# Folding the modulation sums by 24 small matmuls on TensorE in place of 48 small operations on VectorE, in a four-layer transformer forward pass

## The chip, the cores and the metric

The kernel runs on one core of a Trainium2 chip. The metric is the device time of one execution in microseconds (us), lower is better. Five engines work beside each other and meet only through semaphores: TensorE (PE in the profile, with its weight loads as PEld), VectorE (DVE), ScalarE (ACT), GpSimd (POOL), and SyncE (SP), which issues nearly all DMAs here.

## The reference

A batch of one with 256 tokens of width 1024 goes through two blocks of two layers each. The first block ("one" in the kernel) takes its scales, shifts and gates from a conditioning vector `c`:

```python
cond = jax.nn.silu(c)                                  # 1 x 1024
for l in range(2):
    mod = cond @ ada_w[l] + ada_b[l]                   # 1024 -> 9 * 1024
    sh1, sc1, g1, sh2, sc2, g2, sh3, sc3, g3 = jnp.split(mod, 9, axis=-1)
    hn = _modulate(_rms_norm(h, norm_g[l, 0]), sh1, sc1)
    h = h + 0.5 * g1 * _swiglu(hn, ffn1_w_in[l], ffn1_w_out[l])
    hn = _modulate(_rms_norm(h, norm_g[l, 1]), sh2, sc2)
    z = hn @ w_in[l]     # four mixers: differential attention, convolution, gated MLP, forgetting attention
    h = h + g2 * (mixed @ w_out[l])
    hn = _modulate(_rms_norm(h, norm_g[l, 2]), sh3, sc3)
    h = h + 0.5 * g3 * _swiglu(hn, ffn2_w_in[l], ffn2_w_out[l])
```

The second block ("two") has two layers of attention of three kinds and an MLP, with no such modulation. Everything is float32. The change is in how `mod` is summed up, in block one alone.

## The kernel before

**Layout.** The activations `h` lie with the model's 1024 channels on the partitions, as 8 tiles of 128 x 256 tokens. A vector of 1024 numbers, such as `sh1`, is then 8 columns of 128. `mod` of one layer is 72 such columns: 0 to 16 are `sh1, sc1`, 16 to 48 `g1, sh2, sc2, g2`, 48 to 64 `sh3, sc3`, 64 to 72 `g3`.

**Weight products.** Weights stream from HBM in chunks of 256 columns into a ring of four slots. To multiply float32 numbers in TensorE's faster float32r form, ScalarE rounds each chunk into `w_hi` (L1217), GpSimd subtracts it from the original into `w_lo` (L683), each in two halves, and TensorE does three matmuls, hi by hi, hi by lo and lo by hi, for each tile (L717). Two chunks' worth of `w_hi` and `w_lo` are held, so a half is rounded as soon as TensorE has used the one two chunks before. The lines L748 to L752 are the same product for the first chunks of a stage, where it goes tile by tile as the normed input appears.

**Stages of a layer of block one**, in this order: `f1` in (22 chunks in 11 pairs, p = 0 to 10), `f1` out (16 chunks, g = 0 to 3), `z` (the products for the four mixers, 12 chunks), the mixers themselves, `o` (4 chunks), `f2` in and `f2` out. Between two stages stands a norm: `norm_sum` on TensorE (L833, L836) sums the squares, ScalarE takes the root (L1251, L1253), and `scale_norm` on VectorE (L1703, L1712) and ScalarE (L1277) make the normed tiles `hn` and `hn_lo` one by one, 8 of them, for which TensorE waits. Each engine runs its own program in a fixed order written out by hand, and waits on counters such as `vector_done`.

**The modulation.** `ada_w` comes in chunks of 512 columns (2 MB). But for the first four of layer 0, VectorE multiplies and adds a chunk over its 8 tiles (`partial_sum`, L1608 to L1613), transposes 32 x 32 blocks (L1624) and reduces them (L1626), which leaves 16 columns in `ada_columns` in which four groups of 32 partitions hold four partial sums of each output. These must still be added across the groups. `ADA_BATCHES` puts the chunks in three batches a layer: chunks 4 to 11, 12 to 15, and 16 to 21 (the last four of these belong to the next layer). `ada_fold` does a batch on VectorE: four copies (L1639) bring each group of 32 partitions to partitions 0 to 31 in `ada_quarters`, four reduces (L1645) add them and write each quarter of the 128 outputs to its own partitions in `ada_folded`. `modulation` (L1659) then adds the bias from `par_all` and writes `mod`. `gated_scale` (L1718) makes `(1 + scale) * gain` of it.

**Where the folds stand.** Batch 0 is folded behind the last pair of `f1` in, batch 1 behind `scale_norm` of `z`, and batch 2 in front of pair 9 of `f2` in. Behind batch 1's fold VectorE has, at the start of `z`: `modulation(48, 64)`, a `gated_scale`, and the splitting of the forget gate's small weights, `wf_parts` and then `wf_hi` and `wf_lo` in full (L1898, L1900, L1903). Modulation columns 0 to 16 of layer 1 are added at the start of that layer, behind `f2` out of layer 0, just before `gated_scale(0, 8)` and `scale_norm("f1")`.

The bank of PSUM numbered 7 is used by the first chunks' sums (`ada_reduce`, L846, four float32 matmuls a chunk with one column each), by the convolution's taps in `z` and by the heads' outputs in the attention. A float32 matmul stands in the trace as two records, each with a weight load of its own: the eight matmuls of `ada_reduce` are 16 records of L846.

Of the kernel before, what the change touches and what calls it, by code (L numbers as in the profile page):

```python
# [20 lines left out]
ALU = mybir.AluOpType  # L21
ACT = mybir.ActivationFunctionType
AX = mybir.AxisListType
# [34 lines left out]
def constant_tables():  # L58
# [3 lines left out]
    def put(name, a):  # L62
        at[name] = sum(p.shape[1] for p in parts)
        parts.append(np.asarray(a, np.float32).reshape(P, -1))
# [6 lines left out]
    put("group32", r[:, None] // 32 == r[None, :] // 32)  # L71
    put("group64", r[:, None] // 64 == r[None, :] // 64)
    put("neg_suffix", -(r[:, None] >= r[None, :]).astype(np.float32))
    put("neg_ones", -np.ones((P, P)))
# [165 lines left out]

def ada_place(c):

    return (c + ADA_CHUNKS if c < ADA_FIRST else c) - ADA_FIRST

# [139 lines left out]
def build(nc, dram, out, at, old):  # L385

    plan = Plan()
    with ExitStack() as ctx:
# [22 lines left out]
        ident_r, unseen = sb("ident_r", P, dtype=F32R), sb("unseen", P, dtype=F32R)  # L411
        arena_start = sb("arena_start", 48)
        arena = sb("arena", ARENA)
# [19 lines left out]
        ada_columns = view(ARENA - 2048, sum(n for _, n in ADA_BATCHES) * 16)  # L433
        ada_quarters = view(ARENA - 2048 + 288, 4, 128)
        ada_folded = view(ARENA - 2048 + 800, sum(n for _, n in ADA_BATCHES) * 4)
        wf_hi, wf_lo = rounded("wf_hi", 0, KT, P), rounded("wf_lo", KT * P, KT, P)
# [261 lines left out]
        def _(pe):  # L698
# [140 lines left out]
            def ada_reduce(layer, c):  # L839
# [7 lines left out]
                last.then_inc(ada_reduced, 1)  # L847

            pe.wait_ge(tables_in, 32)
            turn(bank[:, 4, 0:KT], rows_c[0:KT], "c turned")  # L850
# [45 lines left out]
            def ffn(s, layer, following):  # L896
                for p in range(PAIRS):
                    for r in range(2):
                        b = bank[:, 2 * (p % 2) + r].rearrange("p (c s) -> p c s", c=2)
                        free = ((silu_done, f"{s} hi {p - 2}") if r else (parts_done, f"{s} gated {p - 2}"),)  # L900
                        product(s + "in", (2 * p + r,), (b[:, 0], b[:, 1]), first=s if p == r == 0 else None,
                                free=free if p >= 2 else ())
                for g in range(4):
                    out_product(s + "out", tuple(range(4 * g, 4 * g + 4)), gated,
                                (bank[:, out_bank(g, 0), 0:S], bank[:, out_bank(g, 1), 0:S]), f"{s} out {g}",
                                ((vector_done, f"h {following} {2 * g - 4}"), (vector_done, f"h {following} {2 * g - 3}"))
                                if g >= 2 else ((parts_done, f"{s} gated {PAIRS - 2}"),) if g == 0 else (),
                                f"{s} gated {PAIRS - 1}" if g == 0 else None)
# [89 lines left out]
            for layer in eng.layers("one"):  # L998
# [3 lines left out]
                ffn("f1", layer, "z")  # L1002
                norm_sum("z")
                if layer == 0:
                    pe.wait_ge(params_in, 16 * n_params_total)
# [589 lines left out]
        def _(dve):  # L1595
# [19 lines left out]
            def ada_sum(layer, c):  # L1615

                loads = (ADA_CHUNKS * layer + c - ADA_FIRST) // 2 + 1
                dve.wait_ge(ada_in[c % 2], 16 * loads)
                dve.wait_ge(vector_done, eng.at())
                n, place = ada_sums(layer, c), ada_place(c)  # L1620
                part, turned_ = bank[:, 5 + c % 2], bank[:, 6 - c % 2]
                partial_sum(n, ada[:, c % 2], part, part)
                dve.wait_ge(ada_summed, n + 1)
                dve.transpose(turned_, part).then_inc(vector_done, eng.step())  # L1624
                dve.wait_ge(vector_done, eng.at())
                dve.tensor_reduce(ada_columns[:, 16 * place:16 * (place + 1)],  # L1626
                                  turned_.rearrange("p (b r) -> p b r", r=32), AX.X, ALU.add) \
                    .then_inc(vector_done, eng.step(f"ada columns {place + ADA_FIRST}"))

            def ada_fold(layer, batch):  # L1630

                c, n = ADA_BATCHES[batch]
                if batch == 2 and layer + 1 == L:
                    n = 2
                place = c - ADA_FIRST
                dve.wait_ge(vector_done, eng.at(f"ada columns {c + n - 1}"))
                for q in range(4):
                    dve.tensor_copy(ada_quarters[0:32, q, 0:16 * n],  # L1639
                                    ada_columns[32 * q:32 * q + 32, 16 * place:16 * (place + n)]) \  # L1640
                        .then_inc(vector_done, eng.step())
                dve.wait_ge(vector_done, eng.at())
                terms = ada_quarters[0:32, :, 0:16 * n].rearrange("p g (x q) -> p q x g", q=4)
                for q in range(4):
                    dve.tensor_reduce(ada_folded[32 * q:32 * q + 32, 4 * place:4 * (place + n)], terms[:, q],  # L1645
                                      AX.X, ALU.add).then_inc(vector_done, eng.step())
                dve.wait_ge(vector_done, eng.at())

            def modulation(layer, first, last):

                if layer == first == 0:
                    dve.wait_ge(ada_reduced, 2)
                    dve.wait_ge(tensor_done, eng.at("first ada 3"))
                    sums = bank[:, 7, MOD_TILES:MOD_TILES + last]
                else:
                    place = 4 * ada_place(first // 4)
                    sums = ada_folded[:, place:place + last - first]
                tt(mod[:, first:last], sums, par_all[:, layer, first:last], ALU.add) \  # L1659
                    .then_inc(vector_done, eng.step())  # L1660
                dve.wait_ge(vector_done, eng.at())
# [59 lines left out]
            def ffn(s, gate_at, layer, following):  # L1721
                for p in range(PAIRS):
                    j = p % 2
                    if (s, p) == ("f2", 9):
                        ada_fold(layer, 2)
                        modulation(layer, 64, 72)
                    of = ada_chunk(s + "in", p, layer)
# [9 lines left out]
                if s == "f1":  # L1737
                    ada_fold(layer, 0)
                    modulation(layer, 16, 48)
                ts(der[:, 24:32], mod[:, gate_at:gate_at + 8], 0.5, None, ALU.mult) \  # L1740
# [123 lines left out]
            for layer in eng.layers("one"):  # L1864
                par = par_all[:, layer]
                if layer:
                    dve.wait_ge(vector_done, eng.at())
                modulation(layer, 0, 16)
                gated_scale(0, 8, R_NORM_G).then_inc(vector_done, eng.step())
# [22 lines left out]
                scale_norm("z", lambda k: col(der, 8 + k), 24)  # L1892
                ada_fold(layer, 1)
                modulation(layer, 48, 64)
                gated_scale(16, 56, R_NORM_G + 16).then_inc(vector_done, eng.step())
# [251 lines left out]
```

## Time and profile before

| | |
|---|---|
| time, median of 3 runs | 1983.54 us (1981.48 to 1986.21) |
| the profiled execution's own time | 1986.21 us |
| span of its trace | 1984.4 us |
| PE busy | 96% of the span |
| POOL busy | 69% |
| ACT busy | 48% |
| DVE busy | 44% |

The span runs from the first to the last instruction that the profiler saw; the execution's own time has 1.8 us around it. A busy share says how long an engine had an instruction in it, not how well it used it. Which engine sets the time at a given place is read from the chain of waits: the list, in order of time, of what the last instruction of all was waiting for, followed back to the start.

### The profile page before, as it was taken

The page shows a single profiled execution, that of the slowest core. Times are in us where ns is not written, and L with a number is a line of the kernel's source. Part 1 is how long each engine was busy: PE and PEld are TensorE (multiplying, and loading weights), DVE is VectorE, ACT ScalarE, POOL GpSimd, SP SyncE. Part 2 cuts the span into 40 slices and gives each one's busy share as a digit, 9 for nine tenths or more (in the row PEclk, how much of TensorE's full clock was granted, in tenths as well). Part 3 has the DMA queues.
Part 4 walks back from the last instruction along what each step waited for, and adds up shares of the span by engine and source line. Part 5 has one row for each costly group of instructions (what it writes and reads, how often), then busy time and mean ns, then how long its engine had stood idle before and what let it go on. Part 6 is the DMA issues. An engine that isn't in the chain of part 4 may idle for free.

```text
span 1984.4 us, 36368 instructions
## 1 busy us (share of the span) xinstructions
PE 1908.5 (96%) x15280; PEld 1836.0 (93%) x15280; DVE 880.9 (44%) x1785; ACT 960.8 (48%) x1491; POOL 1362.3 (69%) x628
## 2 busy tenths in 40 slices
PE   6999997999999999889999999999999999999999
PEld 3999995899999998869999998989999999999999
DVE  3675587374137578745121633143311623243322
ACT  2544455344454445444444445646544445646543
POOL 0888770388878887316888865537897865537896
PEclk8999998999999999989999999999999999999999
DMA  9999650595579896317555653436664643346662
GB/s 317 357 347 310 223 191 23 196 367 191 175 268 367 300 304 189 106 44 270 189 161 169 210 168 119 137 122 198 194 210 149 212 149 128 128 147 192 194 204 94
DMA packets 357075, 397.90 MB, mean 201 GB/s; under 512 B 9016, under 2 KB 319024, under 8 KB 356912
## 3 DMA queue, kind: packets, MB, share of 16 engines
q1 hardware_dynamic: 356752, 395.38, 60.1%
q8 instruction: 120, 1.97, 0.4%
q14 instruction: 43, 0.35, 0.1%
q10 hardware_dynamic: 160, 0.20, 0.0%
HBM read 394.51 MB, written 1.05 MB: 199 GB/s over the span
## 4 chain that ended last, share of the span: by engine, by line
PE 88%; DVE 4%; ACT 3%; POOL 1%; SPq 1%; issue 1%; DMA 1%; DVEq 0%; ACTq 0%
PE bank L717 75%; PE bank L803 3%; PE bank L1140 2%; POOL w_lo L683 1%; PE bank L934 1%; PE bank L974 1%; SPq L545 1%; PE bank L748 1%; PE bank L752 1%; PE bank L749 1%; DVE arena L1776 1%; PE bank L708 1%; ACT arena L1353 1%; DVE bank L1703 1%; DMA arena<-in_ada_w 1%
## 5 line engine op out<-in xcount | busy, mean ns | idle before, releaser
L683 POOL TENSOR_TENSOR w_lo<-ring,w_hi 128x1024 fp32r<-128x1024 f32 (+2 forms) x624 | 1362.1, 2210 | 607.2 <-ACT w_hi L1217 606.5
L1217 ACT ACTIVATE w_hi<-ring 128x1024 fp32r<-128x1024 f32 (+2 forms) x624 | 595.2, 978 | 408.0 <-PE bank L717 370.7
L717 PE MATMUL bank<-hn,w_hi 128*128 128x256 f32 x2752 | 774.6, 281 | 4.0 <-POOL w_lo L683 3.0
L717 PE MATMUL bank<-hn_lo,w_hi 128*128 128x256 f32 x2752 | 766.9, 279 | 0.0
L717 PE MATMUL bank<-hn,w_lo 128*128 128x256 f32 x2752 | 766.9, 279 | 0.0
L717 PEld LDWEIGHTS bank<-hn,w_hi 128*128 128x128 f32 x2752 | 519.5, 189 | 8.0 <-POOL w_lo L683 4.8
L717 PEld LDWEIGHTS bank<-hn_lo,w_hi 128*128 128x128 f32 x2752 | 519.2, 189 | 1.1 <-issue 0.5
L717 PEld LDWEIGHTS bank<-hn,w_lo 128*128 128x128 f32 x2752 | 519.6, 189 | 0.0
L717 PE MATMUL bank<-gated,w_hi 128*128 128x256 f32 x1408 | 247.2, 280 | 0.0
L717 PEld LDWEIGHTS bank<-gated,w_hi 128*128 128x128 f32 x1408 | 215.2, 189 | 0.0
L717 PE MATMUL bank<-gated,w_lo 128*128 128x256 f32 x704 | 197.2, 280 | 0.0
L717 PE MATMUL bank<-up,w_hi 128*128 128x256 f32 x1024 | 174.2, 276 | 0.0
L1611 DVE SCALAR_TENSOR_TENSOR bank<-arena,cond,bank 128x512 f32<-128x512 f32 x204 | 154.2, 756 | 7.3
L717 PEld LDWEIGHTS bank<-up,w_hi 128*128 128x128 f32 x1024 | 154.2, 188 | 0.0
L717 PE MATMUL bank<-up,w_lo 128*128 128x256 f32 x512 | 141.3, 276 | 0.0
L717 PEld LDWEIGHTS bank<-gated,w_lo 128*128 128x128 f32 x704 | 133.1, 189 | 0.0
L1732 DVE TENSOR_TENSOR bank<-arena,bank 128x512 f32<-128x512 f32 x44 | 30.6, 696 | 189.1 <-PE bank L717 189.1
L1305 ACT ACTIVATE arena<-bank 128x512 f32<-128x512 f32 x44 | 26.4, 599 | 162.6 <-PE bank L717 162.2
L1353 ACT ACTIVATE arena<-arena,stat 128x128 f32<-128x128 f32 x120 | 53.2, 444 | 89.8 <-DVE stat L1790 39.8
L717 PEld LDWEIGHTS bank<-up,w_lo 128*128 128x128 f32 x512 | 96.1, 188 | 0.0
L1776 DVE CUSTOM_DVE_ANT_0 arena<-bank,const 128x128 f32<-128x128 f32 x120 | 37.5, 354 | 122.7 <-PE bank L934 119.0
L717 PE MATMUL bank<-w_hi,hn 128*128 128x256 f32 x288 | 83.2, 289 | 0.0
(219 smaller groups left out, 2332.2 us busy)
## 6 DMA issues: line engine op xcount, KB each, us to landing
ring<-in_ffn_w_in SPq DMA_DIRECT2D x88, 1024.0 KB, 7.4
ring<-in_w_in SPq DMA_DIRECT2D x72, 1024.0 KB, 5.1
arena<-in_ada_w SPq DMA_DIRECT2D x35, 2048.0 KB, 10.6
ring<-in_w_up SPq DMA_DIRECT2D x32, 1024.0 KB, 5.4
ring<-in_w_down SPq DMA_DIRECT2D x32, 1024.0 KB, 5.1
ring<-in_ffn_w_out SPq DMA_DIRECT2D x32, 768.0 KB, 4.8
ring<-in_ffn_w_out SPq DMA_DIRECT2D x32, 640.0 KB, 4.1
ring<-in_w_in SPq DMA_DIRECT2D x16, 512.0 KB, 3.6
```

Source lines behind the costliest of these rows:

```text
L545: sp.dma_start(dst, src).then_inc(rows_in, 16)
L683: pool.tensor_tensor(w_lo[:, q, ks], ring[:, r, k0:k0 + n], w_hi[:, q, ks], ALU.subtract) \
L708: i = pe.transpose(dst, src, ident[0:n, 0:n])
L717: last = mm(out, a, b, start=start and i == 0, stop=stop and i == 2)
L803: last = mm(outs[c], ring[:, s, k, c * P:(c + 1) * P], x[:, k, :], start=not begun and j == 0, stop=ends and j == len(ks) - 1)
L1140: last = mm(b[:, c], ring[:, s, k0 + k, c * P:(c + 1) * P], o2[:, k0 + k, :], start=(k == 0), stop=(k == nk - 1))
L1217: f(w_hi[:, q, half * 4:half * 4 + n], ring[:, r, k0:k0 + n], ACT.Copy).then_inc(weights_rounded, 1)
L1305: f(act_tmp[:, j], bank[:, 2 * j], ACT.Silu).then_inc(silu_done, eng.step(f"{s} silu {p}", silu_done))
L1353: f(t, t, ACT.Exp, bias=st[:, b + j:b + j + 1], scale=scale, accum_out=st[:, 10 + 2 * m + j:11 + 2 * m + j]) \
L1611: stt(part, src[:, k], col(cond, k), part, ALU.mult, ALU.add).then_inc(vector_done, eng.step())
L1732: tt(bank[:, 2 * j], act_tmp[:, j], bank[:, 2 * j + 1], ALU.mult) \
L1776: dve.tensor_tensor_reduce(out=tile[:, hd.tp[m][0], c0:c1], in0=bank[:, hd.sb[m][0], c0:c1], in1=tab(mask, c1 - c0, c0), scale=1.0, scalar ...
```

## The change

The eight VectorE operations of a fold go. In their place TensorE does four float32 matmuls: the 128 x 128 stationary operand is a window of a new constant table `fold` of 224 columns, which holds a 32 x 32 identity on each group of 32 partitions between 96 columns of zeros on each side; the four windows put the sum over the groups into output partitions 0 to 31, 32 to 63, 64 to 95 and 96 to 127. The moving operand is a quarter of the batch's columns in `ada_columns` (every fourth; 32, 16, 24 or 8 of them). The results stay in PSUM bank 7, and `modulation` reads them there. TensorE does batch 0 between pairs 9 and 10 of `f1` in, batch 2 between pairs 8 and 9 of `f2` in, and batch 1 behind `norm_sum("z")`. VectorE waits for a new count in `ada_reduced` before it adds the bias.

```diff
+    put("fold", np.concatenate([np.zeros((P, 96)), r[:, None] % 32 == np.arange(32)[None, :], np.zeros((P, 96))], axis=1))
...
-        arena_start = sb("arena_start", 48)
+        arena_start = sb("arena_start", 80)
...
-        ada_quarters = view(ARENA - 2048 + 288, 4, 128)
-        ada_folded = view(ARENA - 2048 + 800, sum(n for _, n in ADA_BATCHES) * 4)
...
+            def ada_fold(layer, batch):
+                c, n = ADA_BATCHES[batch]
+                if batch == 2 and layer + 1 == L:
+                    n = 2
+                last_c = c + n - 1
+                pe.wait_ge(vector_done, eng.at(f"ada columns {last_c}"))
+                place = c - ADA_FIRST
+                sums = ada_columns[:, 16 * place:16 * (place + n)].rearrange("p (x q) -> p q x", q=4)
+                for q in range(4):
+                    last = mm(bank[:, 7, 4 * c:4 * (c + n)], tab("fold", P, 96 - 32 * q), sums[:, q],
+                              start=(q == 0), stop=(q == 3))
+                last.then_inc(ada_reduced, 1)
...
+                    if (s, p) in (("f1", 9), ("f2", 8)):
+                        ada_fold(layer, 0 if s == "f1" else 2)
...
                 norm_sum("z")
+                ada_fold(layer, 1)
...
-            def ada_fold(layer, batch):
...
-                for q in range(4):
-                    dve.tensor_copy(ada_quarters[0:32, q, 0:16 * n],
-                                    ada_columns[32 * q:32 * q + 32, 16 * place:16 * (place + n)]) \
-                        .then_inc(vector_done, eng.step())
-                dve.wait_ge(vector_done, eng.at())
-                terms = ada_quarters[0:32, :, 0:16 * n].rearrange("p g (x q) -> p q x g", q=4)
-                for q in range(4):
-                    dve.tensor_reduce(ada_folded[32 * q:32 * q + 32, 4 * place:4 * (place + n)], terms[:, q],
-                                      AX.X, ALU.add).then_inc(vector_done, eng.step())
-                dve.wait_ge(vector_done, eng.at())
...
-                    place = 4 * ada_place(first // 4)
-                    sums = ada_folded[:, place:place + last - first]
-                tt(mod[:, first:last], sums, par_all[:, layer, first:last], ALU.add) \
+                    dve.wait_ge(ada_reduced, ada_batch(*summed)[1])
+                at_ = MOD_TILES if first == 0 else first
+                tt(mod[:, first:last], bank[:, 7, at_:at_ + last - first], par_all[:, layer, first:last], ALU.add) \
```

The three calls of `ada_fold` on VectorE are removed, and the calls of `modulation` name the chunk on which they depend. The constant table grows by 224 columns (112 KB over all partitions); it is among the tables that are loaded during the first pairs of `f1`.

## Rows read from the trace of the kernel before

**Rows 1.** The page: busy time of the engines, then the chain by engine.
```profile
PE 1908.5 (96%) x15280; PEld 1836.0 (93%) x15280; DVE 880.9 (44%) x1785; ACT 960.8 (48%) x1491; POOL 1362.3 (69%) x628
PE 88%; DVE 4%; ACT 3%; POOL 1%; SPq 1%; issue 1%; DMA 1%; DVEq 0%; ACTq 0%
```

**Rows 2.** Chain of waits: start, length (us), engine, line; f2 layer 0, f1 layer 1.
```profile
388.68 180.92 PE bank L717 x1536
...
581.67 174.70 PE bank L717 x1536
```

**Rows 3.** Stretches: busy us of PE, PEld, DVE, ACT, POOL; PEclk, DMA share, GB/s.
```profile
100.00:180.00 80.00, 80.00 (x681) 80.00 (x681) 47.63 (x69) 37.75 (x45) 66.81 (x30) 1.00 1.01 337
...
620.00:700.00 80.00, 80.00 (x708) 80.00 (x708) 49.67 (x70) 38.39 (x46) 70.17 (x32) 1.00 0.96 328
```

**Rows 4.** Chain of waits: float32 matmuls, two groups with full records.
```profile
44.18 0.98 PE bank L846 x8
...
1237.04 0.85 PE bank L934 x4
```

**Rows 5.** Timeline of DVE, last pairs of f1 in, layer 0.
```profile
151.47 0.69 DVE L1626 TENSOR_REDUCE arena<-bank 128x16 f32<-128x512 f32 x1
...
163.69 0.70 DVE L1732 TENSOR_TENSOR bank<-arena,bank 128x512 f32<-128x512 f32 x1 [9.11 <-PE bank L717]
```

**Rows 6.** Chain of waits: starts of z in layer 0 and of block two.
```profile
238.10 0.71 PE bank L836 x2
...
247.54 7.40 POOL w_lo L683 x5
...
1100.69 7.42 POOL w_lo L683 x5
```

**Rows 7.** Timeline of PE at the start of z, layer 0.
```profile
240.98 0.52 PE L748 MATMUL bank<-hn,w_hi 128*128 128x256 f32 x1 [2.19 <-ACT hn L1277]
```

**Rows 8.** Timeline of DVE behind `scale_norm` of z, layer 0.
```profile
247.38 4.00 DVE L1639 COPY arena<-arena 32x64 f32<-32x64 f32 x4
...
252.62 2.34 DVE L1659 TENSOR_TENSOR mod<-arena 128x16 f32<-128x16 f32 x1
254.99 2.31 DVE L1718 SCALAR_TENSOR_TENSOR der<-mod,arena 128x8 f32<-128x8 f32 x1
...
257.65 0.69 DVE L1903 CAST wf_hi<-wf_parts 128x1024 fp32r<-128x1024 f32 x1
```

**Rows 9.** DVE group: busy us, mean ns of one | idle before, releaser.
```profile
L1732 DVE TENSOR_TENSOR bank<-arena,bank 128x512 f32<-128x512 f32 x44 | 30.6, 696 | 189.1 <-PE bank L717 189.1
```

**Rows 10.** Timeline of POOL and PE in the place of rows 8.
```profile
247.54 9.74 POOL L683 TENSOR_TENSOR w_lo<-ring,w_hi 128x512 fp32r<-128x512 f32 x6 [7.63 <-ACT w_hi L1217]
...
254.88 2.40 POOL L683 TENSOR_TENSOR w_lo<-ring,w_hi 128x1024 fp32r<-128x1024 f32 x1
...
257.70 2.90 POOL L683 TENSOR_TENSOR w_lo<-ring,w_hi 128x1024 fp32r<-128x1024 f32 x1 [0.42 <-ACT w_hi L1217]
...
254.98 0.39 PE L717 MATMUL bank<-hn,w_hi 128*128 128x256 f32 x1 [0.37 <-POOL w_lo L683]
```

**Rows 11.** Chain of waits, start of layer 1.
```profile
570.14 0.53 DVE mod L1659
...
570.69 2.27 DVE der L1718
```

**Rows 12.** Timeline of ACT and POOL at the start of layer 1.
```profile
571.85 0.39 ACT L1253 ACTIVATE bank<-rstd 128x256 f32<-128x256 f32 x1
...
570.57 2.35 POOL L683 TENSOR_TENSOR w_lo<-ring,w_hi 128x1024 fp32r<-128x1024 f32 x1
```

**Rows 13.** Chain of waits: products that resume behind float32 matmuls.
```profile
267.34 5.65 PE bank L717 x48
...
1211.21 5.46 PE bank L717 x48
...
1365.26 168.67 PE bank L717 x1488
```

More of the change, by code:

```diff
@@ L238, with ada_batch @@
 ADA_BATCHES = ((4, 8), (12, 4), (16, 6))
-def ada_place(c):
-    return (c + ADA_CHUNKS if c < ADA_FIRST else c) - ADA_FIRST
+def ada_batch(layer, c):
+    if c < ADA_FIRST:
+        layer, c = layer - 1, c + ADA_CHUNKS
+    b = 0 if c < 12 else 1 if c < 16 else 2
+    return c - ADA_FIRST, 2 + 3 * layer + b + 1
 def ada_column(c):
@@ L1619, in ada_sum @@
                 dve.wait_ge(vector_done, eng.at())
-                n, place = ada_sums(layer, c), ada_place(c)
+                n, (place, _) = ada_sums(layer, c), ada_batch(layer, c)
                 part, turned_ = bank[:, 5 + c % 2], bank[:, 6 - c % 2]
@@ L1628, in ada_sum, with modulation @@
                     .then_inc(vector_done, eng.step(f"ada columns {place + ADA_FIRST}"))
-            def ada_fold(layer, batch):
[L1633 to L1637, printed above, removed]
-                for q in range(4):
-                    dve.tensor_copy(ada_quarters[0:32, q, 0:16 * n],
-                                    ada_columns[32 * q:32 * q + 32, 16 * place:16 * (place + n)]) \
-                        .then_inc(vector_done, eng.step())
-                dve.wait_ge(vector_done, eng.at())
-                terms = ada_quarters[0:32, :, 0:16 * n].rearrange("p g (x q) -> p q x g", q=4)
-                for q in range(4):
-                    dve.tensor_reduce(ada_folded[32 * q:32 * q + 32, 4 * place:4 * (place + n)], terms[:, q],
-                                      AX.X, ALU.add).then_inc(vector_done, eng.step())
-                dve.wait_ge(vector_done, eng.at())
-            def modulation(layer, first, last):
-                if layer == first == 0:
+            def modulation(layer, first, last, summed):
+                if summed == (0, 3):
                     dve.wait_ge(ada_reduced, 2)
                     dve.wait_ge(tensor_done, eng.at("first ada 3"))
-                    sums = bank[:, 7, MOD_TILES:MOD_TILES + last]
                 else:
-                    place = 4 * ada_place(first // 4)
-                    sums = ada_folded[:, place:place + last - first]
-                tt(mod[:, first:last], sums, par_all[:, layer, first:last], ALU.add) \
+                    dve.wait_ge(ada_reduced, ada_batch(*summed)[1])
+                at_ = MOD_TILES if first == 0 else first
+                tt(mod[:, first:last], bank[:, 7, at_:at_ + last - first], par_all[:, layer, first:last], ALU.add) \
                     .then_inc(vector_done, eng.step())
@@ L1724, in ffn @@
                     if (s, p) == ("f2", 9):
-                        ada_fold(layer, 2)
-                        modulation(layer, 64, 72)
+                        modulation(layer, 64, 72, (layer, 17))
                     of = ada_chunk(s + "in", p, layer)
@@ L1737, in ffn @@
                 if s == "f1":
-                    ada_fold(layer, 0)
-                    modulation(layer, 16, 48)
+                    modulation(layer, 16, 48, (layer, 11))
                 ts(der[:, 24:32], mod[:, gate_at:gate_at + 8], 0.5, None, ALU.mult) \
@@ L1867, in _ @@
                     dve.wait_ge(vector_done, eng.at())
-                modulation(layer, 0, 16)
+                modulation(layer, 0, 16, (layer, 3))
                 gated_scale(0, 8, R_NORM_G).then_inc(vector_done, eng.step())
@@ L1892, in _ @@
                 scale_norm("z", lambda k: col(der, 8 + k), 24)
-                ada_fold(layer, 1)
-                modulation(layer, 48, 64)
+                modulation(layer, 48, 64, (layer, 15))
                 gated_scale(16, 56, R_NORM_G + 16).then_inc(vector_done, eng.step())
```

## The prediction

> **What bounds the kernel now.** I read the page first, then the chain of waits. TensorE has an instruction in it for 96% of the span and holds 88% of the chain; VectorE holds 4%, GpSimd 1% [rows 1]. So an operation removed from VectorE is worth something only where the chain passes through VectorE, and each record added to TensorE has to be placed: inside a stretch that the chain gives to TensorE, or in a gap.
>
> Four long stretches are one piece of TensorE work each, 1536 records of L717 without a break: `f1` and `f2` of both layers. Three last 180.9 us, which is 117.8 ns a record; `f1` of layer 1 lasts 174.7 us, 113.7 ns a record [rows 2]. 
>
> No piece of the chain is a fold's copy or reduce. `modulation` and `gated_scale` are on it at the start of layer 1 [rows 11], and GpSimd is, behind each norm [rows 6].
>
> **The folds on TensorE.** A fold is four float32 matmuls, so eight records with a 128 x 128 weight load each and 8 to 32 columns. The nearest row is the same form with one column: eight records of L846 in 0.98 us, 0.122 us each [rows 4]. A record of L717 with 256 columns takes 0.118 us, so the number of columns hardly counts here; I take 0.98 us a fold. Below: 8 x 0.118 = 0.94. Above: 0.85 us for four float32 records of 128 and 256 columns [rows 4], 1.70 for eight. The Trainium skill, "TensorE: Matmul & The Clock Gate", section "LDWEIGHTS (loading the stationary operand)", gives a weight load as the number of columns over 1.2, in ns: an estimate of 107 ns a record, 0.85 us a fold, and 0.5 us less for the four folds below. The trace agrees within 15%.
>
> Batches 0 and 2 are folded inside a stretch with nothing to hide behind: four folds in all, 4 x 0.98 = **+3.9 us** (3.8 to 6.8).
>
> Does TensorE wait there? The fold of batch 0 needs the columns of chunk 11, which VectorE ends at 152.2; TensorE comes to the fold after pair 9, at 163.6, when VectorE's multiplication of that pair is released [rows 5]. That leaves 11 us. Batch 2's chunks are done two pairs ahead. No wait. VectorE in turn needs the results only behind pair 10 (batch 0) or behind its work on pair 8 (batch 2), about a microsecond or more after TensorE has them. No wait either.
>
> Batch 1 is folded behind `norm_sum("z")`, which ends at 238.81 [rows 6]; TensorE then idles until 240.98 for the first normed tile [rows 7]. 0.98 us fits in 2.17. Cost: **0** in both layers; without that cover, 1.0 us each.
>
> **What VectorE loses.** The copies of batch 1 take 4.00 us for four, with 32 x 64 elements, and `modulation` and `gated_scale` 2.34 and 2.31 us for 16 and 8 columns [rows 8]. These are not work but waiting: they end where GpSimd's subtractions end (254.88 + 2.40 = 257.28, `gated_scale` at 257.30) [rows 8, 10]. The multiplication of `f1` and `f2` has one input in PSUM and takes 0.696 us on average of 44, while GpSimd is busy too [rows 9]. So it is the operations that read SBUF twice, or copy within SBUF, which stand behind GpSimd; and the new `modulation`, with its first input in PSUM, won't. The Trainium skill, "SBUF — State Buffer", section "SBUF: two separate sides", calls this an exclusive lock, held for a whole instruction, between GpSimd and VectorE operations with two SBUF inputs or in a two-port mode. The rows agree, and by that rule a long copy also holds GpSimd up, which is the next term.
>
> Folds 0 and 2 on VectorE end in its own idle time of 9.11 us a pair [rows 5]: removing them gains 0.
>
> At the start of `z` the chain runs through five subtractions of GpSimd, 7.40 us, to a TensorE that has idled 0.37 us for them [rows 6, 10]. Block two has the same five with no copies near, 7.42 us [rows 6]: the small copies cost GpSimd nothing, so their removal gives it nothing. But what stood behind them moves up by about 5 us. `modulation` takes 0.2 us now and ends at 247.7, just after GpSimd has begun (247.54) [rows 10]. Then one operation passes at each end of a subtraction: `gated_scale` at 248.8, `wf_parts` at 250.1 and its remainder at 251.3, and the copy of `wf_hi`, 0.69 us for 1024 elements [rows 8], at 252.5, ahead of the fifth subtraction. What that does to GpSimd can be seen where the copy now falls: 2.90 us instead of 2.40 [rows 10]. So the fifth ends 0.5 us later and TensorE with it: **+1.0 us** for two layers. Between 0, if the copy slips behind the fifth, and 2.0, if `wf_lo`, which then falls on the sixth, makes TensorE wait again; I take the middle, as the sixth has about 0.5 us in hand (it ended at 257.28, wanted at 254.98 plus 24 x 0.118 = 257.8).
>
> **The start of layer 1.** `modulation` goes behind the last `h` at 570.14, stands 0.53 us behind GpSimd, and so `gated_scale` starts at 570.69, just after the next subtraction began at 570.57, and stands 2.27 us, until 572.96 [rows 11, 12]. With `modulation` reading PSUM it ends at 570.31; `gated_scale` is then queued in time for the end at 570.57 and done by 570.7. Next late is the root: ScalarE has it at 572.24 [rows 12], about 0.1 us more to VectorE. So 572.34 instead of 572.98: **-0.6 us**. If `gated_scale` misses the end, 0.
>
> **Tables.** The 112 KB more at 337 GB/s [rows 3] are 0.3 us of DMA time in the first pairs, under TensorE's stretch, which no DMA interrupts: 0. Without that cover, +0.3.
>
> Sum of the plain terms: 3.9 + 0 + 0 + 1.0 - 0.6 + 0 = **+4.3 us**.
>
> **The spacing behind a fold.** Behind a fold 624 records of L717 are left in `f1` (pair 10 and the output product, 96 + 528) and 720 in `f2`. The spacing may change at that point: products that resume behind float32 matmuls go at 117.7 ns (5.65 us for 48) in some places, at 113.8 (5.46 for 48) or 113.4 (168.67 for 1488) in others [rows 13]. I count 25 such places in `z`, the attention of block two and its MLP; 9 have the close spacing. A tail is worth 624 x 4.1 ns = 2.5 us in `f1` and 2.9 in each `f2`. Three of the four tails are now wide and can only gain; that of `f1` in layer 1 is close and can only lose. At 9 in 25 the likeliest is that one of three gains (-2.9, 0.44 as worked out from 3 x 0.36 x 0.64 x 0.64) and that layer 1's `f1` loses (+2.5, 0.64). Together -0.4: the likeliest total is 4.3 - 0.4 = **+3.9 us**.
>
> That is 1984.4 + 3.9 = 1988.3 for the span and 1986.21 + 3.9 = 1990.1 for the profiled execution. That execution was the slowest of the three; against their median, 1983.54, it is **1987.4 us**.
>
> **The rivals.**
> - *All tails wide.* No `f2` tail and not `f1`'s of layer 0 gains, and layer 1's loses: 4.3 + 2.5 = +6.8, 1990.3. For it: in `z`, all eight resumptions are wide. Against: 9 of 25.
> - *Tails mostly close.* Two gain and layer 1's loses (4.3 - 5.8 + 2.5 = +1.0), or one gains and layer 1's keeps (+1.4): about 1984.8.
> - *Faster.* The same mechanism on the other side: the break that a fold makes lets TensorE find the close spacing each time. Three tails gain, layer 1's keeps: 4.3 - 8.3 = -4.0, 1979.5. It decides from the third tail on; with two it is -1.5. For it: the long product behind `norm_sum("up")` is close in both layers. A start of a stretch that changes its spacing too would be worth up to 912 x 4.1 ns = 3.7 us more, either way.
> - *The folds are hidden.* If TensorE's stretches were set by the supply of weights, the 3.9 us would vanish: 1.0 - 0.6 = +0.4, 1983.9. Against: no idle time of TensorE in 1536 records.
> - *The folds drain the array.* At 1.70 us each, 6.8 + 0.4 = +7.2, 1990.7. Against: L846.
>
> **How the numbers follow.** A measurement of this kernel can't tell less than about 0.2%, 4.0 us, from no change. Chances: forecast, +2.5 to +5.5, 0.35; all tails wide 0.20; mostly close 0.25; faster 0.08; hidden 0.05; drained 0.07. The forecast lies on the 0.2% line, so half of it counts as slower: 0.175 + 0.20 + 0.07 = 0.45 slower; 0.175 + 0.25 + 0.05 = 0.47 same; 0.08 faster. Range: from -2 (the "mostly close" case with a start that gains 3) to +8 (all wide, with a somewhat dearer fold or `wf_lo`): 1981.5 to 1991.5; the forecast's own is 1986.0 to 1989.0.
>
> **What would show it.** In the profile after: 48 new records of TensorE, eight to a fold, about 0.98 us from the first to the next L717; L1659 at about 0.17 us everywhere; the copies to `wf_hi` near 252 us into the span and a fifth subtraction of 2.9 us; `gated_scale` of layer 1 done before the root; each long stretch split in two, with its spacings to be read on both sides of the fold. The prediction is wrong if the stretches' spacings change far from the folds, if VectorE sits in front of a fold's result, or if the time comes from a place the change does not touch.

## The result, and the profile after

The changed kernel takes 1987.41 us, median of 21 executions, against 1977.89 us for 21 of the kernel before: a ratio of 1.0053, 95% interval 1.0038 to 1.0068. That is 7.5 to 13.4 us slower, with 10.5 us in the middle. One execution of 6697 us is left out of the ratio. The time forecast was 1987.4 us, but its base was too high (1983.54 us, from three runs, where 21 give 1977.89), and the change that it forecast, +3.9 us, too small. The two misses cancel: that the time is right to 0.1 us is luck. As a change, +10.5 us lies outside the -2 to +8 that the range stood for.

The page after: VectorE's busy time fell from 880.9 to 843.2 us, but its share of the chain did not [rows 1]; TensorE has 48 records more. This profiled execution took 1984.52 us and spans 1982.7 us, 1.7 us less than the profile of before, though the kernel is slower in the median: the profile of before was of the slowest of its 21 executions. So the two pages cannot be subtracted, and the rows have to be read place by place.

```profile
PE 1899.7 (96%) x15328; PEld 1826.5 (92%) x15328; DVE 843.2 (43%) x1737; ACT 960.7 (48%) x1491; POOL 1362.0 (69%) x628
PE 84%; DVE 5%; SPq 3%; ACT 3%; POOL 2%; DMA 1%; issue 1%; DVEq 0%; ACTq 0%
```

The chain of waits after, at the four long stretches (start, length in us, engine, line; L719 is the old L717, L862 the fold, L685 GpSimd's subtraction). Compare [rows 2, 6].

```profile
135.16 11.62 DMA ring<-in_ffn_w_in
...
161.61 0.82 PE bank L862 x8
162.43 73.58 PE bank L719 x624
...
237.03 0.71 PE bank L838 x2
...
246.48 8.28 POOL w_lo L685 x5
...
254.80 11.17 PE bank L719 x96
...
389.47 92.48 PE bank L719 x816
481.95 0.80 PE bank L862 x8
482.75 84.89 PE bank L719 x720
...
578.77 103.36 PE bank L719 x912
682.13 0.82 PE bank L862 x8
682.95 73.57 PE bank L719 x624
...
908.91 92.48 PE bank L719 x816
1001.39 0.79 PE bank L862 x8
1002.18 84.90 PE bank L719 x720
```

A reader should divide. 92.48 us for 816 records is 113.3 ns each, 103.36 for 912 the same; 84.89 for 720 and 73.57 for 624 are 117.9. Each of the last three stretches goes into its fold at the close spacing and comes out at the wide one; the granted clock is 1.00 on both sides. The tail of the first is wide too; ahead of its fold this stretch has waited for weights, as the DMA's row shows, which it had not in the profile of before [rows 3]. The fold itself takes 0.79 to 0.82 us.

VectorE after, at the start of `z` in layer 0 (timeline: start, length, engine, line, operation; L1660 is `modulation`, L1719 `gated_scale`), and TensorE's first record behind GpSimd's fifth subtraction:

```profile
246.32 0.17 DVE L1660 TENSOR_TENSOR mod<-bank,arena 128x16 f32<-128x16 f32 x1
246.51 1.26 DVE L1719 SCALAR_TENSOR_TENSOR der<-mod,arena 128x8 f32<-128x8 f32 x1
247.70 0.17 DVE L1896 CAST wf_parts<-arena 128x32 fp32r<-128x32 f32 x1
...
249.10 1.72 DVE L1901 CAST wf_hi<-wf_parts 128x1024 fp32r<-128x1024 f32 x1
250.73 1.79 DVE L1901 CAST wf_lo<-wf_parts 128x1024 fp32r<-128x1024 f32 x1
```
```profile
254.80 0.38 PE L719 MATMUL bank<-hn,w_hi 128*128 128x256 f32 x1 [1.09 <-POOL w_lo L685]
```

`modulation` is 0.17 us long instead of 2.34, and both long copies, not one, now fall ahead of GpSimd's fifth subtraction; TensorE has idled 1.09 us for it instead of 0.37 [rows 8, 10]. From the end of `norm_sum` to the end of the first 96 records behind the subtraction it is 28.24 us (237.74 to 265.98) where it was 27.67 (238.81 to 266.48, where a float32 matmul of 0.86 us begins, ahead of the row at 267.34) [rows 6, 13]. Layer 1 shows the same: 28.24 us where it was 27.69.

The start of layer 1 after:

```profile
568.19 0.17 DVE L1660 TENSOR_TENSOR mod<-bank,arena 128x16 f32<-128x16 f32 x1
568.40 0.29 DVE L1719 SCALAR_TENSOR_TENSOR der<-mod,arena 128x8 f32<-128x8 f32 x1
570.40 0.88 DVE L1704 SCALAR_TENSOR_TENSOR bank<-h,der,bank 128x256 f32<-128x256 f32 x2 [1.71 <-ACT bank L1274]
```

`gated_scale` is done 1.7 us before ScalarE has the root, where it was 0.7 us late [rows 11, 12]. TensorE idles 2.18 us here instead of 2.82.

### The profile page after: what moved, and what is told of

It is laid out like the page before. It is cut to its first block, busy times and chain, and to the rows that moved or that the text cites. A ratio compares the mean times of both kernels' runs of the same rounds, so it can differ in the third digit from the quotient of the medians.

```text
span 1982.7 us, 36417 instructions
## 1 busy us (share of the span) xinstructions
PE 1899.7 (96%) x15328; PEld 1826.5 (92%) x15328; DVE 843.2 (43%) x1737; ACT 960.7 (48%) x1491; POOL 1362.0 (69%) x628
## 4 chain that ended last, share of the span: by engine, by line
PE 84%; DVE 5%; SPq 3%; ACT 3%; POOL 2%; DMA 1%; issue 1%; DVEq 0%; ACTq 0%
PE bank L719 71%; PE bank L805 3%; POOL w_lo L685 2%; PE bank L1161 2%; PE bank L954 1%; PE bank L994 1%; SPq L580 1%; SPq L547 1%; DVE bank L1704 1%; DVE arena L1775 1%; ACT w_hi L1238 1%; PE bank L754 1%; PE bank L750 1%; SPq L590 1%; SPq L544 1%
## 5 line engine op out<-in xcount | busy, mean ns | idle before, releaser
L685 POOL TENSOR_TENSOR w_lo<-ring,w_hi 128x1024 fp32r<-128x1024 f32 (+2 forms) x624 | 1361.8, 2207 | 605.7 <-ACT w_hi L1238 604.9
L719 PE MATMUL bank<-hn,w_hi 128*128 128x256 f32 x2752 | 772.0, 281 | 8.7 <-POOL w_lo L685 7.8
L719 PE MATMUL bank<-hn,w_lo 128*128 128x256 f32 x2752 | 764.3, 278 | 0.0
L719 PE MATMUL bank<-hn_lo,w_hi 128*128 128x256 f32 x2752 | 764.3, 278 | 0.0
L719 PEld LDWEIGHTS bank<-hn,w_hi 128*128 128x128 f32 x2752 | 518.9, 189 | 13.2 <-POOL w_lo L685 7.2
L719 PEld LDWEIGHTS bank<-hn_lo,w_hi 128*128 128x128 f32 x2752 | 518.3, 188 | 1.0 <-issue 0.5
L719 PEld LDWEIGHTS bank<-hn,w_lo 128*128 128x128 f32 x2752 | 518.0, 188 | 0.0
L719 PE MATMUL bank<-gated,w_hi 128*128 128x256 f32 x1408 | 248.9, 281 | 0.0
L719 PEld LDWEIGHTS bank<-gated,w_hi 128*128 128x128 f32 x1408 | 216.7, 190 | 0.0
L719 PE MATMUL bank<-gated,w_lo 128*128 128x256 f32 x704 | 198.0, 281 | 0.0
L719 PE MATMUL bank<-up,w_hi 128*128 128x256 f32 x1024 | 174.2, 276 | 0.0
L719 PEld LDWEIGHTS bank<-up,w_hi 128*128 128x128 f32 x1024 | 154.1, 188 | 0.0
L719 PE MATMUL bank<-up,w_lo 128*128 128x256 f32 x512 | 141.4, 276 | 0.0
L719 PEld LDWEIGHTS bank<-gated,w_lo 128*128 128x128 f32 x704 | 132.2, 188 | 0.0
L719 PEld LDWEIGHTS bank<-up,w_lo 128*128 128x128 f32 x512 | 96.1, 188 | 0.0
L719 PE MATMUL bank<-w_hi,hn 128*128 128x256 f32 x288 | 83.5, 290 | 0.0
```

Of the source, the lines that this page charges most:

```text
L685: pool.tensor_tensor(w_lo[:, q, ks], ring[:, r, k0:k0 + n], w_hi[:, q, ks], ALU.subtract) \
L719: last = mm(out, a, b, start=start and i == 0, stop=stop and i == 2)
```

## The experiments

Each row is a kernel with 12 executions timed (8 in `e4_only_stream`), beside the kernel before on the same chip. The last column is the middle and the 95% interval of the ratio of the times, in us; it need not be the difference of the two medians.

| kernel | median | before | change, us |
|---|---|---|---|
| e1_break32 | 1986.63 | 1978.66 | +5.7 (1.6 to 10.1) |
| e2_break256 | 1984.47 | 1978.66 | +7.7 (3.8 to 11.9) |
| e3_only_z | 1982.74 | 1978.66 | +3.4 (-0.8 to 7.5) |
| e4_only_stream | 1990.63 | 1978.66 | +11.1 (6.5 to 15.8) |
| e5_pause | 1984.63 | 1976.53 | +7.5 (3.6 to 11.3) |
| e6_r32 | 1983.88 | 1976.53 | +8.3 (4.9 to 11.7) |
| e7_fold_pause | 1977.43 | 1976.53 | +0.6 (-4.0 to 5.3) |
| e8_copies_later | 1985.24 | 1976.53 | +7.1 (2.8 to 11.3) |
| e9_both | 1978.99 | 1977.67 | +1.0 (-4.4 to 6.1) |
| e10_pause_first | 1983.82 | 1977.67 | +8.1 (4.4 to 12.1) |
| e11_early | 1987.20 | 1977.67 | +7.3 (2.2 to 12.3) |
| e12_again | 1977.96 | 1978.59 | -0.2 (-4.9 to 4.6) |

**Only a break.** The kernel before, with four float32 matmuls of 32 constant columns where the folds would stand:

```diff
+                    if (s, p) in (("f1", 9), ("f2", 8)):
+                        for q in range(4):
+                            mm(bank[:, 7, 128:128 + 32], ones, const[:, 0:32], start=True, stop=True)
```

> The kernel before with four float32 matmuls of 32 constant columns at the four places of batches 0 and 2 on TensorE, their result read by nobody; folds stay on VectorE. Theory (a short break in the product makes the rest of the stretch go at the wide spacing, 117.8 ns a record, whatever it was before): 8 records are 0.8 us a place, 3.2 us in all, and the tails of 624 and 720 records are wide in all four stretches; where a stretch is close (113.4) in the kernel before, 2.5 to 3.2 us are lost. Over many runs about 8 to 10 us slower than before. Rival (the spacing of a tail is drawn anew, or stays as it was): 3.2 us slower, and at least one close tail in the profile.

The chain of waits, the second and fourth long stretches (the third is 103.36 us for 912 records and 73.57 for 624):

```profile
390.22 92.48 PE bank L717 x816
...
483.51 84.89 PE bank L717 x720
...
910.37 96.11 PE bank L717 x816
...
1007.28 81.71 PE bank L717 x720
```

Two close starts (113.3 ns) go wide (117.9); the one wide start (117.8) comes out close (113.5). The middle of the slowdown, 5.7 us, is over half of the changed kernel's, with no fold, no new wait and VectorE untouched. It is short of the 8 to 10 us expected, and its interval reaches down to the rival's 3.2; what speaks against the rival is the rows, and the times of the next two kernels. If they stand, the loss is not in what the fold computes or who waits for it.

**One long float32 matmul in its place**, 256 columns, `range(1)` and `const[:, 0:256]` in the lines above.

> The same, but one float32 matmul of 256 columns at each of the four places: two records, 0.43 us a place, 1.7 us in all. If only records shorter than their weight load bring the wide spacing, the tails stay close and it is 1.7 us slower than before; if any float32 record does, as much as with 32 columns less 1.5 us: 6 to 8 us slower.

It holds TensorE 0.43 us at a place instead of 0.80 (391.72 + 92.48 = 484.20; the tail starts at 484.63), and the kernel is 3.8 to 11.9 us slower, where the records' own time is 1.7 us. Both tails behind close starts are wide (the fourth stretch as the second).

```profile
391.72 92.48 PE bank L717 x816
...
484.63 84.81 PE bank L717 x720
```

**Eight float32r matmuls of 32 columns**, the type of the stream itself, to see whether float32 is what disturbs it:

```diff
+                        for q in range(8):
+                            mm(bank[:, 7, 128:160], hn[:, q, 0:P], hn[:, q, 0:32], start=True, stop=True)
```

> The kernel before with eight float32r matmuls of 32 columns (one record each, as the product's own are) at the four places, result read by nobody. If float32 records are needed to end the close spacing, the tails keep their start's spacing and it is 3 to 3.8 us slower. If short records do it, the tails behind close starts are wide and it is 8 to 10 us slower.

All three stretches that DMA leaves alone start close and end wide, and 4.9 us, the least that the interval allows, is more than the 3 to 3.8 of the matmuls alone. So the type is not the cause.

```profile
577.98 103.36 PE bank L717 x912
...
682.14 73.59 PE bank L717 x624
```

**The two halves of the change.** One kernel folds batch 1 alone on TensorE and leaves 0 and 2 on VectorE, the other the reverse.

```diff
-                    if (s, p) in (("f1", 9), ("f2", 8)):
-                        ada_fold(layer, 0 if s == "f1" else 2)
...
+                        dve_fold(layer, 2)
...
+                    dve_fold(layer, 0)
```

> The changed kernel with batches 0 and 2 folded on VectorE again and only batch 1 on TensorE, in its gap behind norm_sum of z. Theory: nothing breaks the long stretches, so they may run close from end to end; left is the copy of wf_hi in front of GpSimd's fifth subtraction at z, 0.6 us a layer: 1.2 us slower than before, 9 us faster than the changed kernel. Rival (z or the new table is dear): near the changed kernel.

```diff
-                ada_fold(layer, 1)
...
+                dve_fold(layer, 1)
```

> The changed kernel with batch 1 folded on VectorE again, batches 0 and 2 on TensorE. Theory: all of the loss but the 1.2 us at z is here, less the 0.9 us at the start of layer 1: 9 us slower than before, and all four tails wide. GpSimd's five subtractions at z back at 7.4 us. Rival: near the kernel before.

The folds inside the stretches carry the loss (+11.1 us), with all four tails wide and GpSimd's five subtractions at 7.38 us. Of the other half, folded in TensorE's gap, the profile shows the delay of GpSimd (8.27 us); its +3.4 us does not exclude zero. Its chain, with unbroken stretches at either spacing:

```profile
247.29 8.27 POOL w_lo L687 x5
...
582.19 180.91 PE bank L721 x1536
...
917.04 174.08 PE bank L721 x1536
```

**The spacing is drawn anew in each execution.** The kernel before, unchanged, profiled once more.

> The kernel before, unchanged, profiled and timed once more. Theory (each long stretch starts anew at one of the two spacings, close in roughly 7 of 10 cases, and what the first profile showed was an unlucky draw): the four stretches of 1536 records are not all at the same spacing as in the first profile (117.8, 117.8, 113.7, 117.8 ns a record); at least one of the three that were wide is close, about 174 us instead of 181, and stays so to its end, as there is no break in it. The times scatter by some 8 us either way, with a median within 0.2% of the other runs of the same kernel. Rival (the spacing belongs to the program, its addresses and its order): the same stretches are wide and close as in the first profile.

```profile
390.06 180.92 PE bank L717 x1536
...
583.99 174.35 PE bank L717 x1536
909.94 174.08 PE bank L717 x1536
```

The last stretch was 180.91 us in the first profile and is 174.08 here, in the same kernel. The second and third are as they were, wide and close. The three stretches add up to 529.4 us against 536.5 in the first profile, and the spans differ by 6.3 us (1978.1 and 1984.4). The executions of this one program spread from 1971 to 1989 us; the spacing could explain most of that, but only profiled executions show it.

**Only a pause.** The kernel before, with TensorE waiting at the four places until VectorE has multiplied the pair, and no record added:

```diff
+                    if (s, p) in (("f1", 9), ("f2", 8)):
+                        pe.wait_ge(vector_done, eng.at(f"{s} mult {p}"))
```

> The kernel before, and at the four places TensorE only waits for VectorE's multiplication of the pair just computed: no new record, a pause of about 0.9 us each. Theory A (float32 or short records are what ends the close spacing): the tails behind the pause keep the spacing of their start; 3.6 us slower. Theory B (any break draws the spacing anew, and a break in a close stretch leaves it wide): tails wide, 3.6 us and another 4 to 6 us slower.

```profile
389.41 92.49 PE bank L717 x816
...
482.75 81.91 PE bank L717 x720
```
```profile
482.75 0.39 PE L717 MATMUL bank<-hn,w_hi 128*128 128x256 f32 x1 [0.86 <-DVE bank L1734]
```

Behind 0.86 us of idleness the tail stays close (113.8 ns); of the three stretches that start close, two do. The time is more than that explains: four breaks of 1.02 us, from where the next record was due (481.73) to where it starts, are 4.1 us, the tails should give a little back, and 7.5 us (3.6 to 11.3) were measured. The middle of it is not accounted for. The execution that was profiled, 1980.37 us, is the second fastest of the twelve, with a median of 1984.63, so others may have had more wide tails.

**A pause behind the fold.** The changed kernel with the same wait behind `ada_fold`:

```diff
                         ada_fold(layer, 0 if s == "f1" else 2)
+                        pe.wait_ge(vector_done, eng.at(f"{s} mult {p}"))
```

> The changed kernel with the same pause behind each fold in a stretch. If the pause lets TensorE find the close spacing again, each tail gains 2.5 to 2.9 us and pays about 0.2 us, since the fold already fills most of the pause: 8 to 10 us faster than the changed kernel. If not, 1 us slower than it, tails wide.

Level with the kernel before (+0.6 us), where the changed kernel is 10.5 above it, though TensorE does all of the changed kernel's work and waits besides. In the profile three of the four tails are close, that of the first stretch among them.

**The copies out of GpSimd's way.** The changed kernel with `wf_parts`, `wf_hi` and `wf_lo` moved behind the convolution's input ("conv in"):

```diff
-                for i, whole in enumerate((wf_hi, wf_lo)):
...
                    ALU.mult).then_inc(vector_done, eng.step("conv in"))
...
+                for i, whole in enumerate((wf_hi, wf_lo)):
```

> The changed kernel with the forget gate's small copies (wf_parts, wf_hi, wf_lo) moved behind the multiplication that opens the convolution. Theory: GpSimd's five subtractions at z are back at 7.4 us from 8.28, and TensorE starts 0.9 us sooner in both layers: 1.2 to 1.8 us faster than the changed kernel, which a time of this many runs can hardly show; the profile's row decides.

```profile
248.12 7.39 POOL w_lo L685 x5
```

The five subtractions are back at 7.39 us, so the copies had delayed them. All tails stay wide and the time is no measurable step from the changed kernel's: about a microsecond is below what this can tell.

**Both repairs.**

> The changed kernel with both repairs: TensorE waits for a VectorE result behind each of the three kinds of fold inside a stretch, and the three long copies of the weights stand behind the causal convolution's input, out of GpSimd's way. Theory (the loss is the spacing behind a fold, and GpSimd's delay at the start of z): the five subtractions of GpSimd take about 7.4 us again instead of 8.3, at least two of the four tails of the long stretches keep the close spacing of 113 to 114 ns, and the time is about 1 us under the kernel with the pause alone (1977.4), so 1975 to 1979, which is level with the kernel before (within 0.2%). Rival (the pause alone was a lucky draw of the spacing): as the changed kernel less 1 us, 1985 to 1987, slower than before by 0.3 to 0.5%.

The edit waits at the same four folds as the kernel with the pause alone. The chain, second stretch (the fourth is the same, the third 103.36 and 71.01 us), and TensorE's timeline at its break:

```profile
387.24 92.50 PE bank L719 x816
...
480.58 81.89 PE bank L719 x720
```
```profile
479.56 0.96 PE L862 MATMUL bank<-arena,const 128*128 128x24 f32 x8
480.58 0.39 PE L719 MATMUL bank<-hn,w_hi 128*128 128x256 f32 x1
```

The last three stretches are close before and behind the fold, and the first is close behind it (71.01 us for 624). The pause is short: the product resumes 1.02 us behind the fold's first record, where the changed kernel does after 0.80 (481.79 to 482.59). The added 0.22 us keeps 2.6 to 3.0 us of a tail. The result is level with the kernel before, not faster.

**The pause in front of the fold** instead of behind it, so that the fold's short records still stand directly before the product:

```diff
+                        pe.wait_ge(vector_done, eng.at(f"{s} mult {p}"))
                         ada_fold(layer, 0 if s == "f1" else 2)
-                        pe.wait_ge(vector_done, eng.at(f"{s} mult {p}"))
```

> The changed kernel with TensorE's wait for VectorE in front of each fold instead of behind it. Theory A (short records right in front of the stream's next product leave it at the wide spacing, whatever stood before them): the tails are wide, 117.8 ns a record, and the time is that of the changed kernel plus up to 4 x 0.8 us of idle time, 1987 to 1991. Theory B (any pause at the break is enough): at least two tails are close, and the time is 1977 to 1981, about level with the kernel before.

```profile
391.38 92.49 PE bank L719 x816
...
485.79 81.71 PE bank L719 x720
```
```profile
484.72 1.07 PE L862 MATMUL bank<-arena,const 128*128 128x24 f32 x8 [0.86 <-DVE bank L1733]
485.63 0.36 PE L719 MATMUL bank<-hn,w_hi 128*128 128x256 f32 x1
```

The tails are as theory B has them: all three of these are close (113.5 ns). The time is not, and the timeline gives a reason: from where the next record was due (483.69) to the resumed product it is 1.94 us, 0.92 more than with the pause behind, as the wait no longer overlaps the fold. Four times that is 3.7 us, and the delay of GpSimd that this kernel still has is 1.1 more; its median is 4.8 us over that of the kernel with both repairs. Theory A fell: with a wait ahead of the fold the close spacing stays, though the short records still stand next to the product.

**The break early**, at pair 1, so that 1392 records lie behind it instead of 624 or 720:

```diff
+                    if (s, p) in (("f1", 1), ("f2", 1)):
+                        for q in range(4):
+                            mm(bank[:, 7, 128:128 + 32], ones, const[:, 0:32], start=True, stop=True)
```

> The kernel before with four float32 matmuls of 32 constant columns at pair 1 of each long stretch instead of at the middle, so that nearly the whole stretch lies behind the break (some 1,400 records instead of 624 to 720). Theory (the loss is so many ns for each record behind the break): a stretch that would have been close loses up to 4.3 ns x 1,400 = 6 us instead of 2.7 to 3.1; with about 0.7 of the stretches close and little to lose in the first one, where DMA sets the pace, 3 us for the matmuls and 9 to 16 us for the spacing, slower by 0.6 to 1.0%. Rival (the loss is a fixed price of each break): as the same matmuls in the middle, plus 6 to 8 us, slower by 0.3 to 0.4%.

```profile
598.30 164.03 PE bank L717 x1392
...
933.67 157.87 PE bank L717 x1392
```

The stretch ahead of these two was as the first of them, 164.04 us. The whole tail keeps what it has behind the break: 164.0 us at 117.8 ns or 157.9 at 113.4. The two wide ones had started close (16.32 us for their first 144 records), the close one wide (16.96). But the time, +7.3 us (2.2 to 12.3), is that of the rival, a fixed price of each break (+6 to 8 us), and in its middle well under the 12 to 19 us that the theory asks for. That the loss grows with the tail is seen in the trace and not in the times; this stays open.

**The counts.** In 14 profiles the last three long stretches (the first is left out, as it waits for DMA in most) start close in 31 of 42 cases. At the places of the folds, and at pair 1, behind a break without idle time, 15 of 15 close starts went wide, and 3 of 6 wide ones close. Behind one with a pause, 10 of 12 close starts stayed close. The profiled executions of the four kernels with a pause were all among the four fastest of their twelve, so the last count may flatter the pause.

Two things in the same traces limit this. First, an unbroken stretch mostly keeps its spacing, but not always. The close one of the first profile, `f1` of layer 1 with 174.70 us, did not: two windows of the chain of waits, up to 740.6 us and from 741, and TensorE's timeline between them:

```profile
581.67 159.01 PE bank L717 x1403
...
740.95 15.43 PE bank L717 x131
```
```profile
740.63 0.43 PE L717 MATMUL bank<-gated,w_hi 128*128 128x256 f32 x2
740.90 0.28 PE L717 MATMUL bank<-gated,w_lo 128*128 128x256 f32 x1
```

It is 113.3 ns a record for 1403 records and 117.8 for the last 131, and between them two records take 0.27 us instead of 0.23, with nothing put in. One tail of the kernel with one long matmul, 71.71 us for 624, changes over in the same way for its last 129 records.

Second, not every break without idle time loses the close spacing. In block two six float32 records of `norm_sum("up")`, 1.29 us in all, stand in the stream of each layer's MLP, and the 1488 records behind them take 168.66 or 168.67 us, 113.3 ns each, in all 28 cases of the 14 profiles. In 11 of these the records ahead of the break were close, in 17 wide. In layer 0 of the kernel before they were close; its last four float32 records, with the 1488 right behind them in [rows 13]:

```profile
1364.39 0.86 PE bank L836 x4
```

So what counts is not only that there is a break. Those that lost the close spacing take 0.43 to 0.82 us; this one and those with a pause take over 1 us, the one without idle time, the others with it. Its length may be what counts, and not the idle time in it: no kernel here tells the two apart.

## Why the prediction came out as it did

*Where the loss sits was right:* VectorE's work came off the chain only at the start of layer 1, and the folds inside the stretches carry the loss.

*The folds*, 4 x 0.98 = 3.9 us forecast, measured 0.82 + 0.80 + 0.82 + 0.79 = 3.2. The record of L846 was a little dear. The Trainium skill, "TensorE: Matmul & The Clock Gate", section "LDWEIGHTS (loading the stationary operand)", gave 0.85 a fold as an estimate, and the trace agrees within 7%.

*No wait at the fold, batch 1 hidden:* right. No row of the fold waits, and TensorE's idle time for the first normed tile fell from 2.19 to 1.39 us with the fold in it.

*GpSimd's delay*, +0.5 us a layer forecast, measured 0.57 (28.24 less 27.67) and 0.55, 1.1 in all. The mechanism was right and the order one step off: `wf_parts` slipped through the same gap as `gated_scale`, so both copies fell ahead of the fifth subtraction, which ended 0.9 us later (8.28 for 7.40). That the copies caused it is shown by the kernel that moves them. The Trainium skill, "SBUF — State Buffer", section "SBUF: two separate sides", has this as an exclusive lock for an instruction's length, and the trace agrees: copies of 0.69 us [rows 8] stand 1.72 and 1.79 us there.

*The start of layer 1*, -0.6 us, measured -0.64. *Tables*, 0: the reason given, that no DMA interrupts the first stretch, held in the first profile; but the chain runs through DMA there in the profile after, and also in that of the kernel before taken again. What the 112 KB cost was not tried alone.

*The spacing behind a fold*, forecast at -0.4 us, is the step that failed. I treated the tail's spacing as a draw that has nothing to do with what was there before, at 9 in 25, and set it against stretches of which three in four were wide. Both were wrong. The stretches start close in 31 of 42 cases, so that the first profile was an unlucky one of its own kernel; and behind the fold, or matmuls in its place, without idle time a close start always went wide. Nor was 113.7 ns a spacing of its own, but 113.3 and then 117.8. With the counts, a stretch is wide in 11 of 42 cases ahead of any break and in 18 of 21 behind one, 0.60 more often; over 2 x 720 + 624 records at 4.4 ns each (117.9 less 113.5) that is 5.4 us. The first stretch adds nothing to this: its last part was wide in all three profiles that leave it unbroken (180.91 us for 1536 records in the first, 85.04 for the last 720 in the two others). The sum, worked out afterwards, is 3.2 + 1.1 - 0.6 + 5.4 = 9.1 us, against 10.5 (7.5 to 13.4) measured. The rival "all tails wide" had the picture, but with one loss of 2.5 us, read from one profile, where four are to be had.

*What is shown:* matmuls whose result nobody reads, put in the folds' places, turn the same tails wide, and in two of three kernels cost clearly more than their own time; a wait behind each fold, 0.22 us in the rows, brings the changed kernel level with the kernel before, in both kernels that have it. *What is open:* why TensorE has two spacings; why the close one always stands behind the break in block two; whether it is the idle time or the length of a break that counts; why the pause alone cost more than its length; and why the early break did not cost more than the late one.

## What to carry to other kernels

Before an instruction is put into a steady stream, profile the kernel before more than once: if equal stretches have two lengths, one trace cannot tell what the stream stands to lose. An engine that is the bound should not take over work that another does in its idle time, even at 0.8 us a piece, since what the break does to the next 700 records (3 us here) can cost several times the piece. It need not: measure the records on both sides. And where a break must be made, try it at a place where the engine idles anyway, or with a short wait behind it.

## What the runs showed of the hardware

TensorE ran the same product, one weight load and 256 columns a record, at two spacings, 113.3 and 117.8 ns, at a granted clock of 1.00, for up to 1536 records without changing over; in two places it changed over by itself. Two to eight records, of 8 to 256 columns, in float32 or float32r, put in without idle time, took a stream from the first to the second in 15 of 15 cases; six float32 records of 256 columns elsewhere left it at the first in 28 of 28, whatever it was before. An idle time of 0.2 to 0.9 us at the break kept the first in 10 of 12. I had expected that a wait on the engine that sets the time can only cost.
